# A two-block transformer on one core: half of the two-row modulation columns summed over k on VectorE instead of multiplied on TensorE

## The reference, cut to what matters

```python
D_MODEL = 2048
mod = (c_act @ w_mod + b_mod)[:, None, :]          # w_mod: 2048 x 12288
mod_c = (cc_act @ w_mod + b_mod)[None, None, :]
sh1, sc1, gt1, sh2, sc2, gt2 = jnp.split(mod, 6, axis=-1)
csh1, csc1, cgt1, csh2, csc2, cgt2 = jnp.split(mod_c, 6, axis=-1)
h = rmsnorm_2(x, g_norm1) * (1 + sc1) + sh1
hc = rmsnorm_2(ctx, g_norm1) * (1 + csc1) + csh1
```

## Time and profile before

| what | value |
|---|---|
| time, median of 3 runs | 2143.3 us (2142.68 to 2144.27) |
| the profiled execution's own time | 2141.88 us |
| its span from first to last instruction | 2140.1 us |
| mean granted TensorE clock | 0.996 of full |
| TensorE matmuls busy | 2099.3 us (98% of the span) |
| VectorE busy | 1492.3 us (70%) |
| ScalarE busy | 1039.9 us (49%) |
| GpSimd busy | 97.9 us (5%) |
| bytes moved by DMA | 495.78 MB, mean 232 GB/s |

### The profile page before, as it was taken

One profiled execution on the slowest core, in us unless ns is written; L12 is line 12 of the kernel. 1 busy time (PEld: TensorE's weight loads), 2 busy tenths in 40 slices (PEclk: granted clock), 3 DMA queues, 4 the chain that ended last, 5 costly groups with the idle time before them and its releaser, 6 DMA issues.

```text
span 2140.1 us, 28578 instructions
## 1 busy us (share of the span) xinstructions
PE 2099.3 (98%) x9961; PEld 1722.5 (80%) x9961; DVE 1492.3 (70%) x2178; ACT 1039.9 (49%) x1289; POOL 97.9 (5%) x160
## 2 busy tenths in 40 slices
PE   7999999999999999999999999989999999999998
PEld 6777778888887788887888888778888888888886
DVE  5456657877677897787666777567777777775554
ACT  5444435654444454556434555355555555544443
POOL 0000000110001110111000000000000000000000
PEclk9999999999999999999999999999999999999999
DMA  8887768988887989986544437555655655667664
GB/s 314 280 280 273 272 235 298 375 285 283 289 291 275 333 282 385 323 289 198 158 130 121 119 108 252 186 190 175 194 187 176 199 173 181 186 202 241 192 192 142
DMA packets 284840, 495.78 MB, mean 232 GB/s; under 512 B 22830, under 2 KB 114320, under 8 KB 282688
## 3 DMA queue, kind: packets, MB, share of 16 engines
q1 hardware_dynamic: 276176, 467.98, 66.1%
q0 software_dynamic: 8560, 26.41, 4.1%
HBM read 483.68 MB, written 14.83 MB: 233 GB/s over the span
## 4 chain that ended last, share of the span: by engine, by line
PE 50%; DVE 1%; DMA 1%; ACT 0%; issue 0%; ACTq 0%; SPq 0%; DVEq 0%
PE gemm_ps L1892 45%; PE ps L2276 1%; PE ps L2414 1%; PE ps L2345 1%; DMA w_raw<-in_w_out_dram 1%; DVE w_lo L1097 0%; PE ps L2299 0%; PE ps L2298 0%; PE ps L2240 0%; PE ps L2259 0%; PE ps L1960 0%; PE ps L2221 0%; DMA w_raw<-in_w_down_dram 0%; ACT w_hi L666 0%; PE ps L2362 0%
## 5 line engine op out<-in xcount | busy, mean ns | idle before, releaser
L1097 DVE TENSOR_TENSOR w_lo<-w_raw,w_hi 128x1024 fp32r<-128x1024 f32 (+1 forms) x688 | 827.8, 1215 | 465.4 <-ACT w_hi L666 459.1
L666 ACT ACTIVATE w_hi<-w_raw 128x1024 fp32r<-128x1024 f32 (+1 forms) x688 | 712.0, 1051 | 480.4 <-PE gemm_ps L1892 331.0
L1892 PE MATMUL gemm_ps<-w_hi,a_hi 128*128 128x512 f32 (+1 forms) x2176 | 863.4, 397 | 11.4 <-DVE a_lo L1137 7.1
L1892 PE MATMUL gemm_ps<-w_hi,a_lo 128*128 128x512 f32 (+1 forms) x2176 | 846.4, 389 | 0.0
L1892 PE MATMUL gemm_ps<-w_lo,a_hi 128*128 128x512 f32 (+1 forms) x2176 | 845.6, 389 | 0.0
L1892 PEld LDWEIGHTS gemm_ps<-w_hi,a_hi 128*128 128x128 f32 x2176 | 409.8, 188 | 106.1 <-issue 13.2
L1892 PEld LDWEIGHTS gemm_ps<-w_hi,a_lo 128*128 128x128 f32 x2176 | 409.4, 188 | 86.3
L1892 PEld LDWEIGHTS gemm_ps<-w_lo,a_hi 128*128 128x128 f32 x2176 | 410.1, 188 | 80.4 <-issue 1.0
L1794 DVE SCALAR_TENSOR_TENSOR acc<-gp,cw,acc 128x256 f32<-128x256 f32 x344 | 151.3, 480 | 13.8 <-DVE acc L1794 1.4
L1261 DVE SCALAR_TENSOR_TENSOR msum<-mraw,cs,msum 128x1024 f32<-128x1024 f32 x120 | 153.3, 1278 | 2.9 <-DMA mraw<-in_w_mod_dram 2.2
L1892 PE MATMUL gemm_ps<-w_hi,ft_hi 128*128 128x512 f32 x344 | 134.2, 390 | 2.1 <-DVE w_lo L1097 2.1
(11 more groups left out here) (415 smaller groups left out, 1562.9 us busy)
## 6 DMA issues: line engine op xcount, KB each, us to landing
w_raw<-in_w_in_dram SPq DMA_DIRECT2D x336, 512.0 KB, 4.8
mraw<-in_w_mod_dram SPq DMA_DIRECT2D x192, 512.0 KB, 6.4
w_raw<-in_w_up_dram SPq DMA_DIRECT2D x336, 256.0 KB, 3.0
w_raw<-in_w_down_dram SPq DMA_DIRECT2D x84, 512.0 KB, 4.3
w_raw<-in_w_out_dram SPq DMA_DIRECT2D x64, 512.0 KB, 5.5
w_raw<-in_w_up_dram SPq DMA_DIRECT2D x24, 512.0 KB, 5.6
fold_d<-msum POOLq DMA_DIRECT2D x8, 512.0 KB, 4.8
x_d<-xres POOLq DMA_DIRECT2D x2, 2048.0 KB, 9.1
```

Source lines behind the costliest of these rows:

```text
L666: act.activation(w_hi[:, slot, :, 0:n], raw[:, slot, :, 0:n], ACT.Copy).then_inc(hi_done, 1)
L1097: dve.tensor_tensor(w_lo[:, slot, :, 0:n], raw[:, slot, :, 0:n], w_hi[:, slot, :, 0:n].bitcast(F32), ALU.subtract).then_inc(lo_done, 1)
L1892: mm = pe.matmul(out[:, rt, 0:n], x[:, chunk0 + k, rt * P:(rt + 1) * P], w[:, slot, kk, 0:n], start=(k == 0 and part == 0), stop=(k == chu ...
```

## The change

The number of two-row blocks stays eight, but TensorE keeps four of them and VectorE takes the other four.

- TensorE's four blocks are done in halves of eight chunks (`mod_half`), one half at each of the eight old places. They use slots 4 to 7 of `mraw`. SP fetches unit i of half h after the `w_raw` load of unit place(h-1) + 1 + 2i (it was + 7 + i), and waits for `mod_used` of the half before.
- VectorE sums its four blocks chunk by chunk, two rows for each chunk (`block_rows`), into a new buffer `rsum`, in 64 steps that are spread over units 13 to 93. A step stands behind the `w_lo` of its unit. Its weights use slots 0 to 3 of `mraw`, and SP fetches a new unit of them two units after the place of the last step that read the slot, behind a wait for that step (`row_unit`, `sum_used`).
- For each of these blocks POOL stores `rsum` to `fold_d`, folds 128 partitions to four by five DMAs that add, and copies the four to `mod_d`. The first step of the next block waits until `rsum` is stored.
- DVE makes four copies out of PSUM in place of eight, and POOL four stores of rows.

```diff
-PE_MODS = 8
+MOD_BLOCKS = 8
+PE_MODS = 4
+ROW_BLOCKS = MOD_BLOCKS - PE_MODS
+ROW_OPS = 2 * KC
...
-    places = [13 + 21 * m // 2 for m in range(PE_MODS)]
-    for m, place in enumerate(places):
-        after[place // 8, place % 8] = m
-        copies[(place + 2) // 8, (place + 2) % 8 + 2] = m
-        for i in range(BU):
-            if m or i >= SLOTS:
-                at = places[m - 1] + 7 + i if m else 8 + i - SLOTS
-                loads.setdefault((at // 8, at % 8), []).append(BU * m + i)
+    places = [13 + 21 * h // 2 for h in range(2 * PE_MODS)]
+    for h, place in enumerate(places):
+        after[place // 8, place % 8] = h
+        if h % 2:
+            copies[(place + 2) // 8, (place + 2) % 8 + 2] = h // 2
+        for i in range(SLOTS):
+            at = places[h - 1] + 1 + 2 * i if h else 8 + i
+            loads.setdefault((at // 8, at % 8), []).append(SLOTS * h + i)
     return after, loads, copies
+
+def row_places():
+
+    ops, loads = {}, {}
+    steps = ROW_BLOCKS * KC
+    at = [13 + 82 * j // steps for j in range(steps)]
+    for j, u in enumerate(at):
+        ops.setdefault(((u - 2) // 8, (u - 2) % 8 + 2), []).append(j)
+        if j % UK == 0 and j // UK >= SLOTS:
+            fetched = at[j - SLOTS * UK + UK - 1] + 2
+            loads.setdefault((fetched // 8, fetched % 8), []).append(j // UK)
+    return ops, loads
...
+            def mod_unit(h, i):
+
+                if h:
+                    sp.wait_ge(mod_used, SLOTS * (h - 1) + i + 1)
+                else:
                     sp.wait_ge(S("tr_ps"), TR("x"))
                     sp.wait_ge(S("n_ss"), 1)
+                row = UK * (SLOTS * (h % 2) + i)
+                sp.dma_start(mraw[:, SLOTS + i], w_mod[:, row:row + UK, h // 2 * NBLK:(h // 2 + 1) * NBLK]).then_inc(mod_in[SLOTS + i], 16)
+
+            def row_unit(n):
+
+                if n >= SLOTS:
+                    sp.wait_ge(sum_used, 2 * UK * (n - SLOTS + 1))
+                row, col = UK * (n % BU), (PE_MODS + n // BU) * NBLK
+                sp.dma_start(mraw[:, n % SLOTS], w_mod[:, row:row + UK, col:col + NBLK]).then_inc(mod_in[n % SLOTS], 16)
...
+            def row_store(n):
+
+                pool.wait_ge(sum_used, ROW_OPS * (n + 1))
+                pool.dma_start(fold_d, rsum[:].rearrange("p h c -> p (h c)")).then_inc(sum_out, 16)
+                pool.wait_ge(sum_out, 16 * (n + 1))
+                halves(P, 4)
+                m = PE_MODS + n
+                folding(mod_d[:, :, m * NBLK:(m + 1) * NBLK], fold_d[0:4].rearrange("g (r c) -> g r c", r=2), add=False)
...
+            def block_rows(j):
+
+                n, k = j // KC, j % KC
+                dve.wait_ge(mod_in[j // UK % SLOTS], 16 * (j // UK // SLOTS + 1))
+                row = mraw[:, j // UK % SLOTS, j % UK]
+                if j == 0:
+                    dve.wait_ge(S("cs_set"), 1)
+                if k == 0 and n:
+                    dve.wait_ge(sum_out, 16 * n)
+                for r in range(2):
+                    if k == 0:
+                        dve.tensor_scalar(rsum[:, r], row, cs[:, k, r:r + 1], None, ALU.mult).then_inc(sum_used, 1)
+                    else:
+                        dve.wait_ge(sum_used, 2 * j + r - 1)
+                        dve.scalar_tensor_tensor(out=rsum[:, r], in0=row, scalar=cs[:, k, r:r + 1], in1=rsum[:, r],
+                                                 op0=ALU.mult, op1=ALU.add).then_inc(sum_used, 1)
...
+            def mod_half(h):
+
+                if h % 2 == 0 and h:
+                    pe.wait_ge(mod_evac, h // 2)
+                for i in range(SLOTS):
+                    pe.wait_ge(mod_in[SLOTS + i], 16 * (h + 1))
+                for i in range(SLOTS):
                     for kk in range(UK):
+                        k = UK * (SLOTS * (h % 2) + i) + kk
                         g = k % 4
+                        mm = pe.matmul(pD[32 * g:32 * g + 32, :], cs[:, k], mraw[:, SLOTS + i, kk],
                                        start=(k < 4), stop=(k >= KC - 4), skip_group_check=True)
                     mm.then_inc(mod_used, 1)
```

More of the change, by code:

```diff
@@ L194, in sum_places, with MOD_OUT @@
     return ops, loads
+def MOD_OUT(m):
+    return 16 * (4 * m + 6 * (m - 1))
 MOD_AFTER, MOD_LOADS, MOD_COPIES = mod_places()
+ROW_STEPS, ROW_LOADS = row_places()
 SUM_OPS, SUM_LOADS = sum_places()
@@ L260, in build @@
     msum = at("msum", [P, 2, NBLK], F32, 189.5)
+    rsum = at("rsum", [P, 2, NBLK], F32, 181.5)
     tmpT = at("tmpT", [P, 2, UK, T], F32, 193.5)
@@ L437, in of @@
                     for unit_of in MOD_LOADS.get((block, i), ()):
-                        mod_unit(unit_of // BU, unit_of % BU)
+                        mod_unit(unit_of // SLOTS, unit_of % SLOTS)
+                    for unit_of in ROW_LOADS.get((block, i), ()):
+                        row_unit(unit_of)
                     for row in SUM_LOADS.get((block, i), ()):
@@ L464, in _ @@
             sp.dma_start(ext_d, rel_ext).then_inc(S("rel_out"), 16)
-            for i in range(4):
-                mod_unit(0, i)
+            for i in range(SLOTS):
+                row_unit(i)
             units(w_in, 2, NBLK, mod=fetches(1))
@@ L544, in _, with mod_store @@
         def _(pool):
-            with pool.Fori(0, PE_MODS) as m:
+            fold_steps = [0]
+            def mod_store(m):
                 pool.wait_ge(mod_evac, m + 1)
                 for g in range(4):
[L548 to L556, removed]
+                    pool.dma_start(mod_d[g, :, m * NBLK:(m + 1) * NBLK], mrow[32 * g:32 * g + 2, :]).then_inc(mod_out, 16)
+                fold_steps[0] += 64
+                pool.wait_ge(mod_out, fold_steps[0])
             def folding(dst, src, add=True):
@@ L564, in folding, with halves, sum_leaves @@
                 pool.wait_ge(mod_out, fold_steps[0])
-            def sum_folds(n):
[L568 to L573, removed]
+            def halves(rows, last):
+                while rows > last:
+                    rows //= 2
+                    folding(fold_d[0:rows], fold_d[rows:2 * rows])
+            def row_store(n):
[5 more added lines that the diff above has]
+                folding(mod_d[:, :, m * NBLK:(m + 1) * NBLK], fold_d[0:4].rearrange("g (r c) -> g r c", r=2), add=False)
+            def sum_leaves(n):
+                pool.wait_ge(sum_used, ROW_BLOCKS * ROW_OPS + 16 * (n + 1))
+                pool.dma_start(fold_d, msum[:].rearrange("p h c -> p (h c)")).then_inc(sum_out, 16)
+            def sum_folds(n):
+                pool.wait_ge(sum_out, 16 * (ROW_BLOCKS + n + 1))
+                halves(P, 2)
+                cols = mod_d[0, 0:1, MOD_BLOCKS * NBLK + n * SUM_W:MOD_BLOCKS * NBLK + (n + 1) * SUM_W]
                 folding(cols, fold_d[0:1], add=False)
@@ L583, in gate_bias @@
                 pool.dma_start(mod_d[0, 0:1, cols], a["b_mod_2"][:, cols], accum_op=ALU.add).then_inc(S("gt_bias"), 16)
+            for m in range(PE_MODS):
+                mod_store(m)
+                row_store(m)
             sum_store(0)
@@ L1266, in modulation @@
                     mod_copy(MOD_COPIES[block, i])
+                for step in ROW_STEPS.get((block, i), ()):
+                    block_rows(step)
                 for row in SUM_OPS.get((block, i), ()):
@@ L1558, in step @@
                         dve.wait_ge(S("g_la"), 3)
-                        dve.wait_ge(sum_out, 16 * SUMS)
+                        dve.wait_ge(sum_out, 16 * (ROW_BLOCKS + SUMS))
                     me(dve.tensor_scalar(decays(t), ps[:, 0:2], 0.0, None, ALU.min))
@@ L1918, in product @@
                         after(i)
[L1920 to L1926, removed]
+            def mod_half(h):
[3 more added lines that the diff above has]
+                    pe.wait_ge(mod_in[SLOTS + i], 16 * (h + 1))
+                for i in range(SLOTS):
                     for kk in range(UK):
-                        k = UK * i + kk
+                        k = UK * (SLOTS * (h % 2) + i) + kk
                         g = k % 4
-                        mm = pe.matmul(pD[32 * g:32 * g + 32, :], cs[:, k], mraw[:, i, kk],
+                        mm = pe.matmul(pD[32 * g:32 * g + 32, :], cs[:, k], mraw[:, SLOTS + i, kk],
                                        start=(k < 4), stop=(k >= KC - 4), skip_group_check=True)
@@ L1935, in modulation @@
                 if (block, u) in MOD_AFTER:
-                    mod_block(MOD_AFTER[block, u])
+                    mod_half(MOD_AFTER[block, u])
             ROWS = ("ctx", "x1", "x2")
```

25 lines of the change are left out of this document (9 added, 16 removed).

## The result

The changed kernel takes **2211.65 us** (median of 5 runs, 2208.14 to 2214.44), the kernel before 2143.3: the ratio is 1.0319 (95% interval 1.0308 to 1.033), some 68 us slower. The forecast was 2192 in a range of 2154 to 2212, so the time lies inside it, at its very end: 0.35 us inside, with two of the five runs above it. The direction and the main term held; two things were mis-sized, the clock (too little) and the smaller waits (too much). The profiled execution is the slowest of the five, 2214.44 us for a span of 2212.5.

The account below looks back on a forecast made before the run. The prediction took TensorE as the bound, busy 2099.3 of 2140.1 us. From 2141.88 it took 14.3 for matmuls, added 27.3 for SP's waits and 36.0 for smaller waits, then 1.4: 2192 us, range 2154 to 2212.

Parts of the forecast that it names:

- the clock: After each stall, matmuls at 1.2 GHz: no loss in the sum; as a rival 12 us, time 2204 to 2220, chance 0.14.
- the smaller waits: Units 13 to 93: waits uncovered on TensorE once VectorE's lead is lost, 36 us together, between 0 and some 50.
- The matmuls removed: On TensorE, eight halves in place of eight whole blocks: 14.3 us gained.
- SP's waits: SP's queue stands until TensorE's half begins, holding weight loads from unit p + 2 (p: the half's place): seven stalls, 27.3 us.
- (d): Units 33, 54 and 74: next row block's first step waits for the rsum store; 4.7, 1.3 and 1.8, counted 8 us.
- (a) to (c): VectorE's steps delay the logits' chain (a), 8 us, the norm (b), 13 us, and the copy at i = 4 (c), 5 us.
- the rows' loads: SP's wait for the step at unit a holds the load of unit a + 3: about even, counted 2 us.
- VectorE's 83 us of load: Added steps, 60 at 1.33 us and four at some 0.8, raise VectorE's load to 93% of a 244 us stretch.
- VectorE over 90% busy: Sign expected in the profile after, between units 13 and 93, except in the stalls.
- harmless wait: Rival: SP's wait in its queue costs nothing and the matmuls' saving comes through, 2129 us; chance 0.05.
- recovery case: Rival: VectorE recovers after each stall, so only SP's waits count against the saving, 2156 us; chance 0.22.
- The folds: Each row block's five folds and copy on POOL take 26 to 44 us, covered by a row block's some 55.

Follow-up runs that it names:

- e4: Changed kernel without VectorE's four row blocks and with SP's loads for TensorE's halves back at 7 + i units after the half before: 2131.75 us, ratio 0.9938.
- e3: Changed kernel without VectorE's four row blocks (no steps, loads or stores for them), SP's loads for TensorE's halves left at 1 + 2i: 2176.59 us, ratio 1.0156.
- e2: Kernel before, with SP's loads for each modulation block moved from 7 + i to 1 + i units after the block before: 2169.18 us, ratio 1.0114.
- e9: e5 with SP's loads for the rows two units later in its queue: 2131.09 us, ratio 0.9939.
- e1: Changed kernel with SP's loads for TensorE's halves back at 7 + i units after the half before, not 1 + 2i: 2159.36 us, ratio 1.0066.
- e12: Changed kernel with SP's loads for TensorE's halves back at 7 + i and its row loads two units later, still one sum buffer: 2140.81 us, ratio 0.9988.
- e5: e1 with two buffers for the row sums, used in turn: 2149.86 us, ratio 1.0027.
- e11: e7 with row loads two units later and one row's multiply-adds cut to 8 of 512 columns, except in a block's first step: 2130.78 us, ratio 0.9936.
- e7: e5 with VectorE's steps behind the head's work of the same i instead of ahead of it: 2148.17 us, ratio 1.0019.

## Why the prediction was right, and where it was not

*The matmuls removed* (forecast 14.3): 13.4 in e4's trace over units 13 to 92, and 12 to 14 in the medians. A half shows as 16 records; the one in the rows above takes 1.85 us, from 98.60 to 100.45. Right.

*SP's waits* (forecast 3.9 each, 27.3 in all). This is the step that carried the forecast, and it is right in its mechanism, its place and nearly its size. SP's load goes out 99.69 - 98.60 = 1.09 us after the half begins, as counted. In the changed kernel the seven stalls are 3.51, 3.56, 4.83, 3.69, 3.75, 5.64 and 5.21 us, 30.2 in all. The three longer ones are those whose weights landed late: after 6.3, 6.6 and 5.7 us, against 4.5 to 4.7 in the other four, and the last was issued half a microsecond later as well, behind a load for the rows. For the stall of 5.64 SP's load and ScalarE's rounding of it are

```profile
281.65 1.26 SPq L425 DMA_DIRECT2D w_raw<-in_w_in_dram  x1
288.29 1.06 ACT L710 ACTIVATE w_hi<-w_raw 128x1024 fp32r<-128x1024 f32 x1 [13.36 <-DMA w_raw<-in_w_in_dram]
```

The forecast had this spread in its bounds of 2.9 to 7.3 us for a stall. What makes some landings late is not shown. The estimate by the Trainium skill (DMA: Bandwidth & Descriptors, Anatomy of one DMA), 3.2 us for a landing and 1.4 us less for each stall, was not borne out: five of e3's stalls are 3.6 to 3.7, and the weights' loads of the changed kernel landed after 6.1 us in the median from 50 to 400.

*The clock* (forecast 0 in the sum, 12 as a rival at 0.14). **This is the step that failed.** I set a stall of 3.9 us between a row that fell and short waits that didn't, and took the side of the latter. It fell behind each of the seven stalls in e3, behind each of the seven in the changed kernel and behind its three waits for the store as well, the shortest 2.90 us, and behind three stalls of 2.0 to 3.4 us in e2. Of the changed kernel's 83.0 us over e4 in units 13 to 92, 51.2 are idle and 31.8 are not. 88 distances between large matmuls are at half clock, 0.2 each, which is 17.6; with the smaller matmuls it comes to about 25, since the granted clock is at half for some 65 us of the stretch and TensorE stands for 14 of them. Some 0.16 goes for taking up again in each of the 23 units with a wait, and the rest is time around the heads' small matmuls that I can't split. I also counted one stall as one fall of 1.7 us, where in the changed kernel the unit behind a wait is up to 2.9 us longer. By the prediction's own table the time fell into the clock rival's part, 2204 to 2220 at 0.14, and not into the forecast's, 2168 to 2204 at 0.55. The rival had the mechanism and less than half of its size: 12 us, where the clock took about 25 and all that isn't idle is 31.8.

*The smaller waits* (forecast 36). TensorE idles 21 us outside the seven stalls, not 36.
(d) The wait for the store, forecast 8: 5.02, 2.90 and 3.55 at units 33, 54 and 74, 11.5 in all. VectorE's timeline and then TensorE's at unit 33:

```profile
130.54 1.22 DVE L1141 TENSOR_TENSOR w_lo<-w_raw,w_hi 128x1024 fp32r<-128x1024 f32 x1
136.35 0.88 DVE L1303 TENSOR_SCALAR rsum<-mraw,cs 128x512 f32<-128x512 f32 x2 [4.58 <-DMA fold_d<-rsum]
```

```profile
139.85 0.69 PE L2064 MATMUL ps<-cst,qkn 128*128 128x128 f32 x2 [5.02 <-DVE qkn L1229]
141.04 0.77 PE L1953 MATMUL gemm_ps<-w_hi,a_hi 128*128 128x512 f32 x1
```

The store lands 6.6 to 7.8 us after its issue in this trace, longer than the 4.3 to 7.4 of the earlier trace rows; I had taken 6.2 from the last step on.
(a) to (c) and the rows' loads, forecast 28: 9.5. This walk on paper was too pessimistic. The logits' chain (a) shows 0.71 and 0.85 us at units 47 and 79, not 2.9, with 1.48 and 0.89 one unit later. With TensorE itself slowed by the clock behind each stall, VectorE regained part of its lead before the chain came, which the walk, at 2.74 a unit throughout, left out. That this is the reason is argued, not shown.
Nor was what I made the root of these waits, VectorE's 83 us of load, their root. A step takes 1.33 us as forecast (127.70 to 129.03 on VectorE's timeline), and the 120 multiply-adds of 60 steps are 84.5 us of busy time, but e9 shows that this load costs nothing where the queue doesn't wait for it. What cost was SP's wait for the steps, which I had in the sum for 2 us: 18.6 us by e1 less e12, 18.8 by e5 less e9. Whether less work on VectorE would have shortened that wait at its early place is not tested, since the only run with less work, e11, has the late one. The sign "VectorE over 90% busy" failed too: it is busy for 65% of the stretch, and its 212.29 us are 76% even of TensorE's busy time. I compared one hop of that loop with three units of TensorE and stopped at "about even", without asking what it does to the lead over eighty units.

*The rivals.* The harmless wait is refuted by e3. The recovery case, 2156, counts the stalls alone, and e3, which has them and no rows, is at 2176.6; its idle time on top of e4 would make it 2160, and the rest is the clock for the most part. The folds were covered: the first store's folds and copy are issued from 136.54 to 156.54, and the next store comes at 220.70.

Term by term the trace has -13.4 + 30.2 + 21.0 + 31.8 = 69.6 us, where the forecast had -14.3 + 27.3 + 36.0 + 0 = 49.0. So the forecast was near for a right main term, and for one error of 32 us too little that was partly met by one of 15 too much. That the time still lies inside the range owes as much to this luck as to the main term.

## What to carry to other kernels

In a queue of loads that is in program order, the place of a load is a promise on two sides: early enough for its user, and late enough that what it waits for has happened when the queue gets there. The queue runs ahead by its ring and by the lead of the engines behind it, seven units here, and a wait put at "one unit after the use" stops every load for six. Look at who the queue itself waits for: when the ring's own release is not by far the largest, as it was with 208 of 212 us before, start with the places of the loads. And price a stall of TensorE at its length plus what comes behind it, half as much again in e3 (14 on 28 us), most of it the clock.

## What the hardware showed that I had not expected

- A stall of 2.0 us can already be followed by matmuls at 1.2 GHz. In e2 the stalls of 2.01 and 2.15 us were, with 8 and 7 distances of 0.43 us, and those of 2.02, 1.99 and 1.99 were not. Other runs are as mixed: stalls of 1.99 us in e5, 2.01 in e12 and 1.85 in e7 (granted clock 0.66 from 275 to 280) were, and those of 2.06 in e12 and 2.24 in e7 were not. So the length of a stall of some 2 us doesn't tell by itself. In the rows of e2 above TensorE runs four matmuls at full clock after taking up work, and the fall comes with the fifth. All seven of e3's, of 3.6 to 5.9 us, were followed by a fall.
- VectorE at 87% busy, with the `w_lo`, the steps, the copies and the heads' work interleaved in one order, fed TensorE without one wait in 258 us (e9).
- A store of 512 KB from 128 partitions to DRAM landed 6.0 to 7.4 us after its issue in e9 and 6.6 to 7.8 in the changed kernel, beside the weights' traffic; the weights' loads of the same size took 5.4 and 6.1 in the median from 50 to 400.
